# Recurrence gates as pairs of 64-row matmuls on the two halves of the array, in a fused two-block layer kernel

## The reference, cut to what matters

```python
xc = conv4(xr) + conv_b                                  # (512 tokens, 1024)
xh = xc.reshape(B, S, 16, 64)                            # 16 heads of 64
r = sigmoid(einsum('bshi,hio->bsho', xh, w_a) + b_a)     # a 64x64 matrix per head
i = sigmoid(einsum('bshi,hio->bsho', xh, w_x) + b_x)
log_a = -8 * r * softplus(-lam);  a = exp(log_a)
h_t = a_t * h_(t-1) + sqrt(-expm1(2 log_a)) * i * xc
```

## Time and profile before

| | |
|---|---|
| median of 3 runs | 2496.38 us |
| profiled execution, its time | 2495.95 us |
| its span (first to last instruction) | 2494.1 us |
| TensorE matmul busy | 2477.0 us (99%), 13266 matmuls |
| TensorE weight load busy | 2137.6 us (86%) |
| ScalarE / VectorE / GpSimd busy | 1037.5 / 1137.9 / 1131.6 us |
| DMA | 258.84 MB, mean 104 GB/s |
| convs, gates, k0, k1 | about 35.7 to 120.2 us of the span |

### The profile page before, as it was taken

One profiled execution on the slowest core, in us unless ns is written; L12 is line 12 of the kernel. 1 busy time (PEld: TensorE's weight loads), 2 busy tenths in 40 slices (PEclk: granted clock), 3 DMA queues, 4 the chain that ended last, 5 costly groups with the idle time before them and its releaser, 6 DMA issues.

```text
span 2494.1 us, 33086 instructions
## 1 busy us (share of the span) xinstructions
PE 2477.0 (99%) x13266; PEld 2137.6 (86%) x13266; DVE 1137.9 (46%) x2339; ACT 1037.5 (42%) x2012; POOL 1131.6 (45%) x651
## 2 busy tenths in 40 slices
PE   9999999999999999999999999999999999999998
PEld 8888898888889888889888888888898888888887
DVE  7682486755415632325144455523232446444313
ACT  7553487742335322235343333333343443333323
POOL 3354355544445554444434445444544434444442
PEclk9999999999999999999999999999999999999999
DMA  5233332245332553322322222223322222222222
GB/s 213 76 102 103 94 84 74 64 161 193 137 130 82 192 196 114 101 95 78 116 78 83 85 81 90 84 86 101 110 93 85 85 76 88 82 85 85 93 96 81
DMA packets 89239, 258.84 MB, mean 104 GB/s; under 512 B 8960, under 2 KB 30208, under 8 KB 88704
## 3 DMA queue, kind: packets, MB, share of 16 engines
q1 hardware_dynamic: 89088, 256.74, 30.9%
HBM read 246.22 MB, written 2.10 MB: 100 GB/s over the span
## 4 chain that ended last, share of the span: by engine, by line
PE 91%; DVE 4%; ACT 3%; issue 1%; POOL 0%; DMA 0%; DVEq 0%; SPq 0%; POOLq 0%; ACTq 0%
PE bank L1829 89%; PE bank L1839 2%; ACT PP L2047 1%; DVE pt_lo L2350 0%; DVE Y L2350 0%; DVE C L2350 0%; DVE PP L2609 0%; ACT pt_hi L2047 0%; DVE nt L2350 0%; ACT Hhi L2047 0%; ACT blkv L2047 0%; ACT blkk L2047 0%; ACT w_hi L2047 0%; DMA XR<-in_x 0%; POOL n L2914 0%
## 5 line engine op out<-in xcount | busy, mean ns | idle before, releaser
L2909 POOL TENSOR_TENSOR w_lo<-w_raw,w_hi 128x1024 fp32r<-128x1024 f32 (+1 forms) x302 | 745.8, 2472 | 862.9 <-ACT w_hi L2047 862.8
L1829 PE MATMUL bank<-Hhi,w_hi 128*128 128x512 f32 (+1 forms) x1652 | 639.2, 387 | 0.0
L1829 PE MATMUL bank<-Hlo,w_hi 128*128 128x512 f32 (+1 forms) x1652 | 632.1, 383 | 0.1
L1829 PE MATMUL bank<-Hhi,w_lo 128*128 128x512 f32 (+1 forms) x1652 | 632.1, 383 | 0.0
L2047 ACT ACTIVATE w_hi<-w_raw 128x1024 fp32r<-128x1024 f32 (+1 forms) x318 | 326.2, 1029 | 133.2 <-DMA w_raw<-in_wa 83.4
L1829 PEld LDWEIGHTS bank<-Hhi,w_lo 128*128 128x128 f32 x1652 | 310.5, 188 | 62.1
L1829 PEld LDWEIGHTS bank<-Hlo,w_hi 128*128 128x128 f32 x1652 | 311.2, 188 | 54.9 <-POOL w_lo L2909 0.5
L1829 PEld LDWEIGHTS bank<-Hhi,w_hi 128*128 128x128 f32 x1652 | 310.9, 188 | 54.0
L2909 POOL TENSOR_TENSOR w_fifth_lo<-w_fifth_raw,w_fifth_hi 128x1024 fp32r<-128x1024 f32 x77 | 190.1, 2469 | 214.5 <-ACT w_fifth_hi L2047 214.5
L1829 PE MATMUL bank<-Hhi,w_fifth_hi 128*128 128x512 f32 x388 | 152.8, 394 | 0.0
L1829 PE MATMUL bank<-Hlo,w_fifth_hi 128*128 128x512 f32 x388 | 151.2, 390 | 0.0
(11 more groups left out here) (413 smaller groups left out, 4834.3 us busy)
## 6 DMA issues: line engine op xcount, KB each, us to landing
w_raw<-in_wb SPq DMA_DIRECT2D x169, 512.0 KB, 3.4
w_raw<-in_wa SPq DMA_DIRECT2D x139, 512.0 KB, 3.4
wm<-in_w_ada SPq DMA_DIRECT2D x48, 512.0 KB, 4.4
w_fifth_raw<-in_wb SPq DMA_DIRECT2D x42, 512.0 KB, 3.4
w_fifth_raw<-in_wa SPq DMA_DIRECT2D x35, 512.0 KB, 3.3
QQ<-Y SPq DMA_DIRECT2D x64, 128.0 KB, 2.4
wa_raw<-in_wb SPq DMA_DIRECT2D x5, 512.0 KB, 6.1
XR<-in_x SPq DMA_DIRECT2D x4, 512.0 KB, 7.7
```

Of the source, the lines that this page charges most:

```text
L1829: return self.e.matmul(o, lhs, rhs, start=start, stop=stop)
L2909: self.e.tensor_tensor(x.lo[:, k:k + n, :], x.raw[:, k:k + n, :], f(x.hi[:, k:k + n, :]), ALU.subtract).then_inc(*w_rest(s, k))
```

## The change

Each gate tile now holds, for one group, `[r of head 0 | i of head 0]` in rows 0 to 63 and `[i of head 1 | r of head 1]` in rows 64 to 127, so that one tile does for a group instead of two. Six matmuls of 64 rows by 128 columns go to it, alternating between the lower and the upper 64 rows, and each half of rows writes its own bank. The two halves of a bank hold r and i, so ScalarE needs four `Tanh` of 64x512 for a group instead of two of 128x512. Gates come two groups at a time, after conv 3, 5, 7 and k1, in banks (0, 1) and (4, 5); the convs and k0, k1 keep banks 6 and 7 until the last gates, then 0 and 1 join again. There are four `xs` buffers instead of three. Waits on the gates' sums name a group alone; the second key product's copies wait for gate 7 instead of gate 6. The weight stream is one slab shorter (8 gate tiles instead of 16).

```diff
         def rnn_gates(self, j):
-            for what in range(2):
-                tile = self.tile()
-                b = self.main.take()
-                names = [("gate", j, what)] + [("slab", tile.s)] * tile.ends
-                self.gate_sums(j, what, banks[b][:, :], tile, self.freed[b], names)
+            for x in range(2):
+                tile, b = self.tile(), ((0, 1), (4, 5))[x]
+                names = [("gate", j + x)] + [("slab", tile.s)] * tile.ends
+                self.gate_sums(j + x, [banks[y][:, :] for y in b], tile, [self.freed[y] for y in b], names)
                 if tile.ends:
                     self.slab_done(tile.s)
-                self.gate_tanh(j, what, banks[b][:, :])
-                self.freed[b] = [act_rnn.by("tanh", j, what)]
-                self.gated[j] = what == 1
-                yield 1
+                for y in range(2):
+                    self.gate_tanh(j + x, y, banks[b[y]])
+                    self.freed[b[y]] = [act_rnn.by("tanh", j + x, y, 1)]
+                self.gated[j + x] = True
+            yield 3
...
-                if gp == 0:
-                    yield from self.rnn_gates(6 + br)
+                if gp == 0 and br:
+                    yield from self.rnn_gates(6)
+                    self.main.which = [6, 7, 0, 1]
...
-            self.main.which, self.wide.which = [6, 7, 0, 1], list(range(8))
+            self.main.which, self.wide.which = [6, 7], list(range(8))
...
-                if j > 1:
-                    self.run(self.rnn_gates(j - 2))
+                if j % 2 and j > 1:
+                    self.run(self.rnn_gates(j - 3))
...
-            x = xs[j % 3]
+            x = xs[j % 4]
             self.wait_ge(tile.h, act_rnn.by("xs", j), bank_free, dve_rnn.by("xs", j), tile.l)
-            self.mm3(o, (tile.hi, tile.lo), (x[0][:, :], x[1][:, :]), True, True).then_inc(*sums.named(*names))
+            for n, (w, v) in enumerate(((tile.hi, x[0]), (tile.hi, x[1]), (tile.lo, x[0]))):
+                for y in range(2):
+                    ins = self.mm(o[y], w[ROWS[y], :], v[ROWS[y], :], n == 0, n == 2)
+            ins.then_inc(*sums.named(*names))
...
-            self.put((TR, TI)[what][:, j, :], o, ACT.Tanh, scale=.5, bias=half[:, 8 * what + j:8 * what + j + 1]).then_inc(
-                *act_rnn("tanh", j, what))
+            for x in range(2):
+                what = (x + y) % 2
+                self.put((TR, TI)[what][ROWS[y], j, :], o[ROWS[x], :], ACT.Tanh, scale=.5,
+                         bias=half[ROWS[x], 8 * what + j:8 * what + j + 1]).then_inc(*act_rnn("tanh", j, y, x))
...
-            self.wait_ge(done, dve_cmp.by("value", 3), sums.by("gate", (5, 6)[br] if gp == 0 else 7, 1))
+            self.wait_ge(done, dve_cmp.by("value", 3), sums.by("gate", 5 if gp == 0 and br == 0 else 7))
```

More of the change, by code:

```diff
@@ L239, in program @@
     xs = [(at(f"xs_hi{i}", o, [128, 512], F32R), at(f"xs_lo{i}", o + 2, [128, 512], F32R))
-          for i, o in enumerate((R0 + 80, R0 + 84, R0 + 88))]
+          for i, o in enumerate((R0 + 80, R0 + 84, R0 + 88, R0 + 92))]
     Y2 = at("Y2", R0, [128, KT, 2, 512], F32R)
@@ L1784, in load_gmlp @@
         def load_gmlp(self):
-            self.wait_ge(sums.by("gate", 7, 1))
+            self.wait_ge(sums.by("gate", 7))
             self.e.dma_start(wst[:, :, :], A["wst"]).then_inc(*wst_in(0))
@@ L1894, in cmp_values, with gate_sums @@
             ins.then_inc(*cmp_sums("value"))
-        def gate_sums(self, j, what, o, tile, bank_free, names):
-            x = xs[j % 3]
+        def gate_sums(self, j, o, tile, bank_free, names):
+            x = xs[j % 4]
             self.wait_ge(tile.h, act_rnn.by("xs", j), bank_free, dve_rnn.by("xs", j), tile.l)
-            self.mm3(o, (tile.hi, tile.lo), (x[0][:, :], x[1][:, :]), True, True).then_inc(*sums.named(*names))
+            for n, (w, v) in enumerate(((tile.hi, x[0]), (tile.hi, x[1]), (tile.lo, x[0]))):
+                for y in range(2):
+                    ins = self.mm(o[y], w[ROWS[y], :], v[ROWS[y], :], n == 0, n == 2)
+            ins.then_inc(*sums.named(*names))
         def mix_sums(self, b, bank_free):
@@ L2101, in conv, with gate_tanh @@
         def conv(self, j, o, done):
-            x = xs[j % 3]
-            self.wait_ge(dve_rnn.by("conv", j, 3), sums.by("gate", j - 3, 1) if j > 2 else
+            x = xs[j % 4]
+            self.wait_ge(dve_rnn.by("conv", j, 3), sums.by("gate", j - 4) if j > 3 else
                          [act_norm.by("h", "first", KT - 1, 1), pool_norm.by("rest", "first", KT - 1, 1)])
             self.put(x[0][:, :], XC[:, j, :]).then_inc(*act_rnn("xs", j))
-        def gate_tanh(self, j, what, o):
-            self.wait_ge(sums.by("gate", j, what), ready0.by("half"), act_norm.by("h", "first", KT - 1, 1),
+        def gate_tanh(self, j, y, o):
+            self.wait_ge(sums.by("gate", j), ready0.by("half"), act_norm.by("h", "first", KT - 1, 1),
                          pool_norm.by("rest", "first", KT - 1, 1))
-            self.put((TR, TI)[what][:, j, :], o, ACT.Tanh, scale=.5, bias=half[:, 8 * what + j:8 * what + j + 1]).then_inc(
-                *act_rnn("tanh", j, what))
+            for x in range(2):
+                what = (x + y) % 2
+                self.put((TR, TI)[what][ROWS[y], j, :], o[ROWS[x], :], ACT.Tanh, scale=.5,
+                         bias=half[ROWS[x], 8 * what + j:8 * what + j + 1]).then_inc(*act_rnn("tanh", j, y, x))
         def rec_decay(self, j):
             x, r = XC[:, j, :], TR[:, j, :]
-            self.wait_ge(dve_rnn.by("start", j), act_rnn.by("tanh", j, 0), dve_soft.by("coefh"))
+            self.wait_ge(dve_rnn.by("start", j), act_rnn.by("tanh", j, 1, 1), dve_soft.by("coefh"))
             self.put(x, r, ACT.Exp, scale=coef[:, j:j + 1], bias=coef[:, j:j + 1]).then_inc(*act_rnn("decay", j))
@@ L2137, in value_split @@
             v = VS[gp][:, t + 1 - n:t + 1, :, :, :].rearrange("p t b o n -> p (t b o) n")
-            self.wait_ge(done, dve_cmp.by("value", 3), sums.by("gate", 7, 1))
+            self.wait_ge(done, dve_cmp.by("value", 3), sums.by("gate", 7))
             self.put(v[:, :, 0:64], banks[b][:, 0:256 * n].rearrange("p (x n) -> p x n", n=64)).then_inc(*act_kqv("v", gp, t))
@@ L2157, in mix_rows @@
         def mix_rows(self, b):
-            self.wait_ge(gmlp_sums.by("rows"), sums.by("gate", 7, 1))
+            self.wait_ge(gmlp_sums.by("rows"), sums.by("gate", 7))
             self.put(rw[:, :, :].rearrange("p g t -> p (g t)"), banks[b][:, :]).then_inc(*act_gmlp("rows"))
@@ L2494, in conv @@
                     *dve_rnn("conv", j, d))
-            h, l = xs[j % 3]
+            h, l = xs[j % 4]
             self.wait_ge(act_rnn.by("xs", j))
@@ L2499, in rec_start @@
         def rec_start(self, j):
-            self.wait_ge(act_rnn.by("tanh", j, 1))
+            self.wait_ge(act_rnn.by("tanh", j, 1, 1))
             self.stt(TI[:, j, :], TI[:, j, :], 1., XC[:, j, :], ALU.add, ALU.mult).then_inc(*dve_rnn("start", j))
@@ L2517, in keys_low @@
         def keys_low(self, gp, br, odd, o):
-            self.wait_ge(act_kqv.by("k", gp, br, odd), sums.by("gate", (5, 6)[br] if gp == 0 else 7, 1))
+            self.wait_ge(act_kqv.by("k", gp, br, odd), sums.by("gate", 5 if gp == 0 and br == 0 else 7))
             self.tt(KS[gp][odd][ROWS[1 - odd], br, :], o[ROWS[odd], :], f(KS[gp][odd][ROWS[odd], br, :]), ALU.subtract).then_inc(
@@ L3023, in layout @@
     qp = q.reshape(1024, 2, 2, 4, 64).transpose(0, 1, 3, 2, 4).reshape(1024, 1024)
[L3025 to L3032, removed]
+    wa, wx = i["rnn_wa"][0].reshape(8, 2, 64, 64), i["rnn_wx"][0].reshape(8, 2, 64, 64)
+    gates = np.concatenate([np.concatenate([wa[:, 0], wx[:, 0]], 2), np.concatenate([wx[:, 1], wa[:, 1]], 2)], 1)
     wm = [mg[:, 1024 * b:1024 * b + 1024] for b in range(3)]
@@ L3035, in layout @@
     seq = [tiles(kc), tiles(vc), part(xr, 0), part(xr, 1)]
-    for j in range(8):
-        seq += [part(xr, j + 2) if j < 6 else part((ks, kw)[j - 6], 0), gates[2 * j:2 * j + 2]]
+    for j in range(0, 8, 2):
+        seq += [part(xr, j + n) if j < 6 else part((ks, kw)[n - 2], 0) for n in (2, 3)] + [gates[j:j + 2]]
     seq += [side_by_side(np.concatenate([vs[:, 0:128], vw[:, 0:128], ng], 1)), tiles(qp[:, 0:512])]
@@ L3067, in layout @@
     par = [i["g_pre_mix"], i["g_post_mix"], i["g_pre_ffn"], i["g_post_ffn"], i["gmlp_ln_g"], i["gmlp_ln_b"],
-           i["rnn_conv_w"], i["rnn_conv_b"], i["rnn_ba"], i["rnn_bx"], i["rnn_lam"],
+           i["rnn_conv_w"], i["rnn_conv_b"], i["rnn_ba"], i["rnn_bx"].reshape(8, 2, 64)[:, ::-1], i["rnn_lam"],
            i["nsa_pe_k"], i["nsa_pe_v"], i["norm_w_2"], i["b_ada_2"], i["ret_gn_w_2"], i["final_norm_w_2"]]
```

## The result

The changed kernel takes **2512.6 us** (median of six runs, 2511.56 to 2513.94) against 2495.81 us (2494.85 to 2496.57) for the kernel before on the same chip: ratio 1.0068, 95% interval 1.0058 to 1.0079. It is slower, as predicted, but by 16.8 us, not 7.4, and outside the range of 2497.5 to 2507. The profiled execution took 2513.68 us, its span 2511.9.

What follows compares the result with a forecast made beforehand. TensorE was taken to bound the kernel, with ScalarE full before the v product. v's wait for gates 7 (+5.9) and the clock (+1.5) added 7.4 to 2495.95, giving 2503.4 us, range 2497.5 to 2507.

Steps and rivals of the forecast that it cites:

- when conv 7 ends: TensorE's end of conv 7, now 105.02: -3.6 - 1.8 + 0.7 + 0.1 = -4.6 us, so 100.4.
- the +0.7 at conv 2: Conv 2 returns to bank 6, which conv 0 had, and starts at 47.55 instead of 46.82.
- the visits' price: Going to 64-row gate matmuls and back costs TensorE about 0.22 us for each of four visits.
- xs_hi(7): ScalarE's rounding for group 7 comes 3.4 us behind the end of conv 7, at 103.8.
- ScalarE's list: From group 7's xs_hi to the last Tanh: 23.4 us instead of 15.68, with 16 pieces at 0.70, ending at 127.2.
- rival (b): Tanh pieces overlap, down to 0.57 us, and the clock hardly costs: 2499.9 us, down to 2496; chance 0.18.
- the 127.35: Start of the v product's tenth matmul, waiting for bank 5 from gates 7, instead of 121.43: +5.9 us.
- rival (c): The 64-row halves don't run side by side; 12 pairs ahead of conv 7's end add 2.7 us: 2506.1; chance 0.12.
- The clock: After TensorE's wait of ten microseconds at v, a lower granted clock costs +1.5 us (0 to 3).
- The rivals: On the faster side: v doesn't wait for gates 7, TensorE keeps its 5.8 us lead, 2490.2 us; chance 0.12.
- theory of two waits: Made after the result: the loss is conv 0's bank wait (5.7 us and some clock) and v's (14.4 us), nothing else of weight.
- the rival's point: Made after the result: moving waits about brings nothing, because another engine is next in line; no chance given.

Runs made afterwards that it cites:

- conv_banks: The changed kernel with convs, k0 and k1 in banks 0 and 1, and each visit's first gates in banks 6 and 7; 2506.8 us.
- serial_halves: The changed kernel with three matmuls of the lower half issued first, then three of the upper, instead of in turn; 2513.24 us.
- late_rec: The changed kernel with the recurrence's elementwise part starting 19 ticks later on the planner's list, behind the last Tanh; 2504.93 us.
- all_fixes: The changed kernel with conv_banks' edit (gates 6 in banks 4 and 5, gates 7 in 6 and 7) and the recurrence started 20 ticks later; 2496.09 us.
- dense5: all_fixes with k1's copies moved behind the last Tanh and the recurrence's steps 5 ticks apart instead of 7; 2495.6 us.

## Why the prediction was wrong

**The step that failed** is "when conv 7 ends". It asked of every conv whether the one before it in the same bank was through, found the +0.7 at conv 2, and said that "the later convs find their bank free". It never asked it of conv 0, because the list of banks starts there; but the turn counter does not. A product of the compression was in bank 6, and the wait with its clock cost 8.1 us. Conv 0 started 5.3 us later than before (40.95 instead of 35.69, the opening of this execution being 0.45 ahead), lost 2.4 to the clock, and the 0.7 at conv 2 did not arise: 7.0 us, against the 6.5 by which conv 7 ended late (106.87 instead of 100.4). conv_banks shows that with conv 0's wait away the step comes out: 100.25. That it does so within 0.15 us is in part luck, for the visits' price in it was half of what it is: four slots of a visit are 0.1 us longer, not two (in serial_halves' rows 73.38 to 73.70, 73.70 to 74.03, 74.96 to 75.29 and 75.29 to 75.63), about 0.4 us a visit instead of 0.22, and something else in the sum was too dear by as much. At the end of the kernel the wait costs 5.8 (taken out) or 6.6 (put in).

**xs_hi(7), undersized.** 5.3 us behind conv 7's end, not 3.4. The 3.4 came from a row in which VectorE stood idle ahead of conv 7's convolution. Two groups' gates now lie between convs, so convs 6 and 7 follow each other without gates; VectorE came to conv 6 at 103.18, behind the compression's small casts, and to conv 7 at 109.01, behind an `xs_lo` of 2.04 us (0.69 for group 6 before). GpSimd computes `w_lo` at that time, from 106.13 to 111.35; whether that is the reason was not tested. In conv_banks the lag is 5.3 again (100.25 to 105.57), so it is not a result of conv 0's wait. Cost: +1.9.

**ScalarE's list, undersized.** 25.8 us (112.20 to 138.02) instead of 23.4. The pieces are right: 0.71 apart, 0.70 predicted, and they don't overlap; rival (b) falls. 1.9 of the 2.4 is idle time inside, at 130.37 for VectorE's `XC`, which the sum put at nothing.

These make v's tenth matmul 6.5 + 1.9 + 2.4 = 10.8 us later than the 127.35 that the prediction had; it started at 138.05, 10.7 later. The span grew by 17.8 instead of 7.4, 10.4 more.

**What held.** Pairs run side by side: 0.233 us each (107.20 to 107.44), 0.227 predicted; rival (c) falls, and so does the thought that they need to be issued in turn. No gate up to 5 waits. v waits at its seventh matmul for a Tanh of gates 7, with a second short wait at the tenth. The Trainium skill's drain at a change of tiling mode ("TensorEngine Tiling (Array Packing)", Key Properties) is no more than these 0.1 us in each of four slots. The Trainium skill's 3.07 of 4 for four row tiles ("TensorE: Matmul & The Clock Gate", Part 3) does not carry over to two: inside a visit the trace shows 2 x 0.227 / 0.233 = 1.95 of 2. The Trainium skill says in "TensorEngine Tiling (Array Packing)", PSUM Bottleneck, that evacuation does not get faster with the array; here it even got slower, and the run with whole Tanh prices the splitting at 4.4 us.

**The clock** after v's wait: matmuls 0.25 us apart instead of 0.139 from the tenth (138.05) until about 141.5, which costs 1.75 us, near the 1.5 predicted. The size is partly luck: it was 2.6 us in late_rec, behind a shorter wait. I had allowed for it there and not at conv 0, where it cost 2.4. A run that keeps TensorE busy through the wait was not made, so the share of the clock rests on rows alone.

**The rivals** on the faster side needed bank 5 by 115.7; it came at 138. The theory of two waits holds up to all_fixes: -5.8 for conv 0's bank and -12 of v's waiting make 17.8 us, and 16.5 came back. That it does not go below the kernel before was the rival's point. The traces show where a lead is lost, in front of ScalarE's square roots at 169 to 172 us. That ScalarE and VectorE have no room at all for TensorE's gain is a reading of these few orders and is not shown.

## What to carry to other kernels

- Where resources are handed out in turn, a change to the list changes who gets which one from the first taker on. Work out the actual bank (or buffer) of every taker near the change, and who had it last, also across the stage's border.
- Fewer cycles on the full engine can be worth nothing if they cost the engine behind it more. Count the evacuation in instructions: here 5.4 us less on TensorE (about 3.7 with the visits' price) were bought with 16 more Tanh, and the eight pieces of the last two gates alone take 5.7 us of ScalarE's list ahead of v's last bank.
- When a wait goes, ask at once what the moved work now stands in front of. Starting the recurrence later freed v and then blocked a weight slab 50 us later.

## What the runs showed of the hardware that was not expected

- Two halves of 64 rows, three matmuls issued for one and then three for the other, still ran side by side, at 0.233 us a pair with 512 fp32r columns.
- Going to 64-row matmuls and back lengthens four starts by 0.1 us each, the one into the first pair, the one behind it, the one out of the last pair and the one behind that: about 0.4 us a visit.
- ScalarE's Tanh pieces of 64 rows by 512 from PSUM follow each other in 0.71 us, pieces of 128 rows in 0.57, although the rows say 0.69 for both: half the rows cost more from start to start, not the same. Why was not tested.
- After standing still for 5.7 us TensorE ran twelve matmuls at 0.43 us (the 1.2 GHz level); after 14.4 us v's matmuls were at 0.25 instead of 0.139 until 5 us behind the restart, and in late_rec, after only 5.2 us, until 6.7 us behind it. In all_fixes2 v's waits of 1.17 and 0.73 us left the granted clock at 1.00 from 115 to 138 us, and in dense5 waits of 1.13 and 0.74 brought it to 0.93: nearly the same waits, with and without a loss of about 1.5 us.
